# RWKV matrices right behind the z tiles, twelve gate tiles instead of fourteen beside the substitution, and a step's small gate operations ahead of the shift rows

## The chip, the cores and the metric

One core of one Trainium2 chip. The metric is the device time of one execution in microseconds, as the median of the runs. The profile is one further execution; its rows give times in us from the start of its span.

## What is computed

One step of a one-layer decoder for 256 new prompt tokens behind 16 meta tokens, and for 8 running sequences with one token each. One input projection `P = rmsnorm(h) @ w_in` feeds two branches. They are merged by sigmoid gates, and a product-key expert mixer (PEER) follows. All is float32.

```python
# DeltaNet branch, in chunks of the sequence
A = strict(kb @ k.T * decay) + I          # unit lower triangular
u, w = solve(A, [v * beta, kb * exp(G)])
v_new = u - w @ S
o = (q * exp(G)) @ S + tril(q @ k.T * decay) @ v_new
S = S * exp(G_last) + (k * exp(G_last - G)).T @ v_new
# RWKV-7 branch, token by token (the kernel solves it in chunks too)
S = S * w + (S @ a) b^T + v k^T ;  y = S @ r
# merge
m = sigmoid(P_gate_a) * (o_dn @ w_up_dn) + sigmoid(P_gate_b) * (o_rw @ w_up_rw)
h = h + m @ w_out
h = h + peer(rmsnorm(h))                  # top 16 of 128 x 128 experts per head, gathered rows
```

Here `g = -exp(a_log) * softplus(alpha + dt_bias)` and `beta = sigmoid(...)` come from eight small columns of the projection. For these the kernel needs `exp` and `log` on a 128 x 16 tile.

## The kernel before

The kernel is written per engine, with semaphores by hand. Each engine has one instruction list in a fixed order. TensorE (`pe`), ScalarE (`act`), VectorE (`dve`) and GpSimd (`pool`) compute, and SyncE (`sp`) issues nearly all transfers in one queue. Line 1428 is the matmul helper, line 1846 the activation helper: nearly all matmuls and activations carry these lines. A float32 matmul appears as two MATMUL records, each with its weight load. The sequence is three chunks of 96 tokens (NCH = 3, TC = 96, with padding), and the 8 sample tokens stand behind them in the same tiles (296 columns, or 264 without padding and meta tokens). PSUM has eight banks, called 0 to 7.

The work around the change, in order:

- **Projections** (`project`, line 1446): tiles of 128 output columns, each 8 matmuls over the 8 slices of the model dimension. Order: r, kr, vr, wag (the RWKV rows), then two q tiles, then 14 transposes that give the last token-shift rows (lines 1487 to 1490), two q tiles, and twelve products of the low-rank gates (lines 1495 to 1501: the first eight read 64 rows of the array, the last four 128). Then come k, v and z, with small matmuls of both branches between.
- **ScalarE at that place** (lines 1880 to 1909): 14 scalings of the RWKV rows (`mix`), copies of the shift rows from banks 4 to 7, tanh and sigmoid of the low-rank inputs (`wag_act`), the first q tile out, exponentials of `gtmp`, `bt`, `alog`, the second q tile out, the logarithm of `gtmp`, two more q tiles, then the sigmoids of the low-rank products. A function that is not in the loaded table needs an ACT_TABLE_LOAD. VectorE makes `gtmp` (lines 2144 to 2148) behind its fourteen parts of `mix`. Its line 2149 waits for the logarithm.
- **Middle** (lines 1549 to 1643). TensorE: z tile 0; the q norms spread back over rows (8-row products); 12 matmuls for the decay matrices (`gb_ready`, banks 4, 5, 7); the k norms spread back; z tile 1; the six DeltaNet matrix pairs (`kq_ready`, banks 0 to 5); six sample transposes (banks 6, 7); six groups of token transposes (banks 6, 7 in turn, so each waits for ScalarE's copy of the one before the last); z tile 2; six groups of RWKV row transposes; z tile 3; then `rw_matrix`: 12 groups with k (`rwm_ready`), half a gate tile, the key sum in bank 7, and 12 groups with b (`rwb_ready`). VectorE masks each result (lines 2286 to 2320). The last six groups need all of `rwb_ready`, as their result overwrites the b vectors.
- **Triangular inverses.** All 36 unit lower triangular matrices of 96 x 96 are inverted. The 32 x 32 diagonal blocks go out through DRAM by SP (`emit_blocks_in`), 108 blocks one per partition. VectorE inverts them by substitution in 31 steps (lines 2331 to 2341). SP brings them back (`emit_blocks_out`: one transfer out, nine in). Around the substitution VectorE runs the two halves of the sample state update `sample_rwkv` (line 602, nine instructions of 128 x 1024). The first needs `svp` (sixteen small transfers of SP, issued once the token rows are copied) and `strw` (two loads behind them, lines 466 to 477). TensorE meanwhile runs the gate tiles of the list `FILL` (line 1260, `fill_tile`, banks 6 and 7 in turn), fourteen of them. ScalarE takes each out through a sigmoid.
- **Coupling** (`inv_turn`, `inv_left`, `inv_once`, `inv_twice`, lines 1652 to 1704): nine units of four matrices join the blocks, pipelined over TensorE, ScalarE and VectorE. Units 0 to 2 are DeltaNet (chunks 0, 1, 2), 3 to 8 RWKV. VectorE makes `inv_c` (line 2350) behind the second half of the sample state.
- **Chunks** (line 1752): chunk after chunk, both branches' states. Chunk 0 begins once all nine units are done (`inv_z_used`). VectorE copies the first right side, `v_dn`, to `r_buf` (line 2445), and with it signals `dn_r_done`. SP waits for that signal before the sixteen small transfers of the sample result (line 501), since these overwrite `v_dn`'s place. Two gate tiles (g3's third and fourth) stand at the end of chunks 0 and 1.
- **Weights.** Slots of 2 MB; g0 to g3 share slot 0. `IN_PARTS` (line 251) cuts g1, g2 and g3 into parts, each of which is fetched as soon as its columns of the tile group before are used.

Behind it follow the merge and the output projection (to about 402 us) and the expert mixer, whose gathers and weighting run to the end of the span.

## Time and profile before

| | |
|---|---|
| three runs, median (lowest to highest) | 1148.66 us (1147.56 to 1153.62) |
| the profiled execution: its time / its span | 1150.32 / 1148.6 us |
| TensorE busy | 982.6 us (86%), x3667 |
| VectorE busy | 706.5 us (62%), x1870 |
| ScalarE busy | 264.1 us (23%), of it 22 table loads 28.2 us |
| GpSimd busy | 521.4 us (45%) |
| mean granted TensorE clock | 0.978 |

The span is the time from the first to the last instruction of the profiled execution. Its time is 1.7 us more. A busy TensorE is modelled from its instructions, and is not TensorE at its peak. The granted clock is given as a share of 2.4 GHz, and has two levels, 1.00 and 0.50.

### The profile page before, as it was taken

How to read it: one execution, taken by the hardware profiler on the slowest of the kernel's cores; microseconds unless marked ns; L12 is line 12 of the kernel's file. 1: busy time of each engine (PE TensorE's matmuls, PEld its weight loads, DVE VectorE, ACT ScalarE, POOL GpSimd, SP SyncE). 2: the span in 40 equal slices, each digit the busy share in tenths (PEclk: the TensorE clock that was granted, in tenths of full speed). 3: DMA queues.
4: the chain of work that ended last, by engine and by line, in shares of the span. 5: the costliest groups of instructions: out<-in, count | busy, mean ns of one | idle time of the engine just before them, and what ended most of it. 6: DMA issues, size and time to landing. Idle time of an engine off the chain costs nothing.

```text
span 1148.6 us, 11115 instructions
## 1 busy us (share of the span) xinstructions
PE 982.6 (86%) x3667; PEld 549.7 (48%) x3667; DVE 706.5 (62%) x1870; ACT 264.1 (23%) x635; POOL 521.4 (45%) x583
## 2 busy tenths in 40 slices
PE   6999998999999998988987777777777777777787
PEld 5886676889987447654442222222222222222221
DVE  2025862983466338883775775776686676677543
ACT  2147544023251012220131111111122111111111
POOL 2000100000000016577577677777767777777763
PEclk9998989998999998998999999999999999999999
DMA  9342022463165319999999999999999999999996
GB/s 288 110 153 74 1 76 50 135 171 82 40 208 208 110 46 405 407 371 353 409 406 403 409 409 409 406 408 408 408 388 410 409 409 410 405 409 404 395 371 263
DMA packets 121862, 334.24 MB, mean 291 GB/s; under 512 B 19119, under 2 KB 36370, under 8 KB 121542
## 3 DMA queue, kind: packets, MB, share of 16 engines
q0 software_dynamic: 76032, 276.86, 61.2%
q1 hardware_dynamic: 45642, 56.64, 15.2%
q8 instruction: 30, 0.49, 0.2%
q14 instruction: 26, 0.21, 0.0%
q10 hardware_dynamic: 132, 0.04, 0.0%
HBM read 326.99 MB, written 5.74 MB: 290 GB/s over the span
## 4 chain that ended last, share of the span: by engine, by line
PE 31%; DMA 28%; DVE 23%; POOL 9%; issue 5%; ACT 3%; ACTq 0%; DVEq 0%; POOLq 0%
PE bank L1428 29%; DMA sb_all<-in_peer_u,idx 22%; POOL sb_all L591 9%; DMA sb_all<-in_peer_v,idx 6%; DVE sb_all L1148 6%; ACT sb_all L1846 2%; DVE sb_all L1126 1%; DVE sb_all L1124 1%; DVE sb_all L1128 1%; DVE sb_all L2337 1%; DVE sb_all L2334 1%; DVE key_i L1096 1%; DVE sb_all L1089 1%; ACT L1846 1%; DVE key_i L1090 1%
## 5 line engine op out<-in xcount | busy, mean ns | idle before, releaser
L1428 PE MATMUL bank<-sb_all 128*128 128x512 f32 (+19 forms) x3390 | 952.3, 433 | 145.8 <-DMA sb_all<-in_peer_v,idx 135.6
L1428 PEld LDWEIGHTS bank<-sb_all 128*128 128x128 f32 (+8 forms) x3390 | 522.9, 182 | 569.7 <-DMA sb_all<-in_peer_v,idx 320.4
L1148 DVE CUSTOM_DVE_ANT_0 sb_all<-sb_all,bank 128x1024 f32<-128x1024 f32 x264 | 314.8, 1220 | 186.5 <-DMA sb_all<-in_peer_u,idx 186.0
L591 POOL DMA_INDIRECT sb_all<-in_peer_u,idx x264 | 252.6, 957 | 212.4 <-issue 161.1
L591 POOL DMA_INDIRECT sb_all<-in_peer_v,idx x264 | 254.6, 965 | 88.8 <-issue 63.8
L1846 ACT ACTIVATE sb_all<-sb_all 128x128 f32<-128x128 f32 (+9 forms) x367 | 145.1, 421 | 561.7 <-PE bank L1428 368.6
L1846 ACT ACTIVATE sb_all<-bank 128x264 f32<-128x264 f32 (+18 forms) x175 | 76.7, 455 | 305.2 <-PE bank L1428 272.0
L627 POOL MEMSET sb_all<- 128x512 f32 x1 | 0.5, 524 | 140.9 <-PE bank L1428 140.9
L1418 POOL MEMSET sb_all<- 128x3456 f32 x1 | 3.0, 2984 | 129.1 <-DVE sb_all L2248 129.1
L2129 DVE SCALAR_TENSOR_TENSOR sb_all<-sb_all 128x288 f32<-128x288 f32 x14 | 6.1, 514 | 61.2 <-ACT sb_all L1846 61.2
L1846 ACT ACT_TABLE_LOAD x22 | 28.2, 1283 | 7.5 <-DVE sb_all L2269 3.9
L1148 DVE DVE_READ_ACCUMULATOR2_ANT sb_all<- 128x1 f32 x264 | 21.7, 82 | 0.0
L2199 DVE SCALAR_TENSOR_TENSOR sb_all<-sb_all 128x288 f32<-128x288 f32 x36 | 16.0, 504 | 6.7 <-ACT sb_all L1846 6.6
L1061 DVE TENSOR_TENSOR sb_all<-sb_all,bank 128x512 f32<-128x512 f32 (+1 forms) x6 | 4.1, 683 | 25.0 <-PE bank L1428 25.0
L1126 DVE TENSOR_TENSOR sb_all<-sb_all 128x864 f32<-128x864 f32 x17 | 18.0, 1059 | 0.6
L1124 DVE TENSOR_TENSOR sb_all<-sb_all 128x864 f32<-128x864 f32 x17 | 18.0, 1059 | 0.6
L1128 DVE TENSOR_REDUCE sb_all<-sb_all 128x16 f32<-128x864 f32 x17 | 17.9, 1055 | 0.6
L1234 DVE SCALAR_TENSOR_TENSOR sb_all<-sb_all 128x1024 f32<-128x1024 f32 x8 | 10.3, 1285 | 12.6 <-DMA sb_all<-in_peer_v,idx 12.6
L2309 DVE TENSOR_TENSOR sb_all<-bank,sb_all 96x192 f32<-96x192 f32 x12 | 4.1, 340 | 19.5 <-PE bank L1428 19.5
L1420 POOL MEMSET sb_all<- 108x1024 f32 x1 | 1.0, 952 | 31.7 <-DVE sb_all L2295 31.7
L1846 ACT ACTIVATE sb_all<-bank,sb_all 96x128 f32<-96x128 f32 (+5 forms) x39 | 13.4, 415 | 6.3 <-PE bank L1428 5.5
L1086 DVE MAX8 sb_all<-sb_all 128x8 f32<-128x128 f32 x34 | 8.2, 284 | 10.5 <-ACT sb_all L1846 10.5
(237 smaller groups left out, 403.5 us busy)
## 6 DMA issues: line engine op xcount, KB each, us to landing
sb_all<-in_w_in SPq DMA_DIRECT2D x8, 2048.0 KB, 8.1
sb_all<-in_peer_wq SPq DMA_DIRECT2D x4, 2048.0 KB, 17.3
sb_all<-in_w_in SPq DMA_DIRECT2D x6, 1024.0 KB, 4.9
sb_all<-in_peer_u,idx POOLq DMA_INDIRECT x264, 10.8
sb_all<-in_peer_v,idx POOLq DMA_INDIRECT x264, 11.0
out<-sb_all SPq DMA_DIRECT2D x8, 512.0 KB, 3.9
sb_all<-in_w_out SPq DMA_DIRECT2D x2, 2048.0 KB, 8.6
sb_all<-in_x_prompt SPq DMA_DIRECT2D x4, 512.0 KB, 4.4
```

Of the source, the lines that this page charges most:

```text
L591: pool.indirect_dma_start(ring[at % 8], None, table[0], bass.IndirectOffsetOnAxis(ap=idx[:, c:c + 1], axis=0)).then_inc(landed[at % 8], 16)
L1089: k(v.match_replace(curm[:, x, :], best[:, x, 0:8], src[:, x, :], NEG))
L1090: k(v.max_index(key_i[:, PT * x:PT * x + 8], best[:, x, 0:8], src[:, x, :]))
L1096: k(v.max_index(key_i[:, PT * x + 8:PT * x + 16], best[:, x, 8:16], curm[:, x, :]))
L1124: k(tt(onehot, iota.unsqueeze(1).broadcast_to([128, PT, NCAND]), row(posf, 128, PT, NCAND), ALU.is_equal))
L1126: k(tt(onehot, onehot, cidx.unsqueeze(1).broadcast_to([128, PT, NCAND]), ALU.mult))
L1128: k(v.tensor_reduce(eidf, onehot, AX, ALU.add))
L1148: v.tensor_tensor_reduce(uring[i % 8], uring[i % 8], x, 1.0, 0.0, ALU.mult, ALU.add, hdot[:, u % 2, j:j + 1]).then_inc(u_free, 1)
L1428: return nc.tensor.matmul(out, lhsT, rhs, start=start, stop=stop, **kw)
L1846: return nc.scalar.activation(out, in_, func, **kw)
L2199: step(stt(x, pre[:, f, j:j + NP], pc("conv", 12 * j + f), x, ALU.mult, ALU.add))
L2334: step(tt(t, ublk[:, 0:k, k].unsqueeze(2).broadcast_to([108, k, n]), vblk[:, k, k:32].unsqueeze(1).broadcast_to([108, k, n]), ALU.mult))
```

## The change

Six things, all in the order of work:

1. **Small gates** (ScalarE, VectorE): VectorE makes `gtmp` ahead of its fourteen parts of `mix`. ScalarE does the three exponentials and the logarithm directly behind its fourteen scalings, ahead of the shift rows, and takes the four q tiles out in one go.
2. **z tile 1** stands between and behind the decay matrices in bank 6, in four pieces of two slices. The sample transposes stand between the DeltaNet matrices. z tile 2 (bank 6) comes ahead of the token transposes, which now go to banks 0 to 5. z tile 3 (bank 7) comes directly behind them.
3. **The RWKV matrices** come directly behind z. The row transposes stand between the second six of them. The first six with b follow; then the key sum, half a gate tile and the last six. VectorE copies the key sum after all of them.
4. **Twelve gate tiles** beside the substitution. g3's first and second tile come behind the coupling loop and in chunk 0 (banks 0 and 3). g3 is fetched whole, once g2 is used and the blocks are back.
5. **Coupling by chunks**: the nine units go chunk by chunk (each DeltaNet and both RWKV). Chunk 0's first product starts after the seventh unit. The last `inv_twice` comes behind gate tile 0.
6. **No copy of the first right side**: TensorE reads `v_dn`; `dn_r_done` counts from chunk 1, so SP's sample result transfers wait for chunk 1.

The diff, cut to its core:

```diff
-        UNITS_INV = [(g, q) for g in range(3) for q in range(3)]
+        UNITS_INV = [(g, q) for q in range(3) for g in range(3)]
...
-        IN_PARTS = {"g1": (256,), "g2": (256,), "g3": (128, 128)}
+        IN_PARTS = {"g1": (256,), "g2": (256,)}
...
             step(fn(view(E + 4096, 2 * NX), view(E + 4096, 2 * NX), ACT.Sigmoid))
+            step(fn(gates(12), gates(12), ACT.Sigmoid))
...
-        FILL = [(name, f) for name in ("g0", "g1", "g2") for f in range(4)] + [("g3", 0), ("g3", 1)]
+        FILL = [(name, f) for name in ("g0", "g1", "g2") for f in range(4)]
...
             for c in range(NCH):
                 for h in range(DH):
                     ins = mm(psv((4, 5, 7)[c], 128, TC, at=TC * h), gbc[0:TC, 4 * c + h, :], incl[0:TC, :])
                 ins.then_inc(gb_ready.sem, 1)
-            for f in range(4):
-                pe.wait_ge(qk_mul.sem, qk_mul.at(f + 1))
-                mm(psv(f, 128, NC), to_rows[0:8, 4 + f, :], qk_norm[0:8, :]).then_inc(k_back.sem, 1)
+                z_tile(1, 6, 2 * c, 2 * c + 2)
+            key_back(0)
+            key_back(1)
+            z_tile(1, 6, 6, KT)
+            key_back(2)
+            key_back(3)
             pe.wait_ge(dec_exp.sem, dec_exp.at(2 * NCH))
-            project("z", T0, banks=4, part=(1, 2))
...
+                if n >= 1:
+                    sample_rows(n - 1)
+            sample_rows(5)
+            pe.wait_ge(svt_ready.sem, svt_ready.at(5))
+            z_tile(2, 6, 0, KT)
             for n in range(6):
-                if n < 2:
-                    pe.wait_ge(svt_ready.sem, svt_ready.at(5 + n))
-                else:
-                    pe.wait_ge(tok_ready.sem, tok_ready.at(n - 1))
+                pe.wait_ge(kq_used, n + 1)
...
+            z_tile(3, 7, 0, KT)
...
-            pe.wait_ge(proj_used, 30)
             for n in range(12):
-                if n >= 6:
+                if n < 6:
+                    pe.wait_ge(tok_ready.sem, tok_ready.at(n + 1))
+                else:
+                    rw_rows(n - 6)
                     pe.wait_ge(rwm_used, n - 5)
                 rw_matrix(n % 6, kb, n // 6, n % 6 // 2, n % 2).then_inc(rwm_ready.sem, 1)
...
+            for n in range(6):
+                pe.wait_ge(rwm_used, n + 7)
+                rw_matrix(n, bb, 0, n // 2, n % 2).then_inc(rwb_ready, 1)
             pe.wait_ge(prw_ready.sem, prw_ready.at(6))
             mm(psv(7, 128, 32), ones, sdv[:, 2, :]).then_inc(kq_sum.sem, 1)
+            fill_tile(0, KT // 2)
+            for n in range(6):
+                pe.wait_ge(rwb_used, n + 1)
+                rw_matrix(n, bb, 1, n // 2, n % 2).then_inc(rwb_ready, 1)
             fill_tile(KT // 2, KT)
...
+            for u in range(NU + 2):
+                if u < NU:
+                    inv_turn(u)
+                if 1 <= u < NU + 1:
+                    inv_left(u - 1)
+                if u >= 2:
+                    inv_once(u - 2)
+                if u >= 3:
+                    inv_twice(u - 3)
+            pe.wait_ge(inv_z_used, 7)
+            right_side(0).then_inc(rw_r, 1)
+            pe.wait_ge(inv_x_used, NU)
+            gate_tile(0, 0)
+            inv_twice(NU - 1)
             for c in range(NCH):
...
                 for h in range(DH):
-                    ins = mm(psv(1, TC, 128, at=128 * h), xTm(4 * c + h), r_buf[0:TC, 128 * h:128 * h + 128])
+                    r_h = r_buf[0:TC, 128 * h:128 * h + 128] if c > 0 else v_dn[0:TC, 0, 128 * h:128 * h + 128]
+                    ins = mm(psv(1, TC, 128, at=128 * h), xTm(4 * c + h), r_h)
                 ins.then_inc(dn_u, 1)
+                if c == 0:
+                    gate_tile(1, 3)
                 pe.wait_ge(rw_r_done, c + 1)
+                pe.wait_ge(inv_z_used, NU)
...
             for f in range(14):
                 fn(mix[:, f, 0:NP], prw[:, f, 1:1 + NP], scale=omu[:, f:f + 1]).then_inc(mix_part.sem, 1)
+            act.wait_ge(ln_done, 1)
+            step(fn(gtmp, gtmp, ACT.Exp, scale=-1.0))
+            step(fn(bt, ba[:, :, 0:4], ACT.Exp, scale=-1.0))
+            step(fn(alog, alog, ACT.Exp))
+            step.sync()
+            fn(gtmp, gtmp, ACT.Ln, bias=1.0).then_inc(ln_done, 1)
...
-            evacuate([pre[:, 0, 3 + PAD:3 + NC]])
...
+            evacuate([pre[:, f, 3 + PAD:3 + NC] for f in range(4)])
...
+                if c == 0:
+                    gate_out(0, 0)
+                    act.wait_ge(inv_sum.sem, inv_sum.at(NU))
+                    gate_out(1, 3)
+                    act.wait_ge(yv_ready, 1)
+                    act.wait_ge(strw_sent, 32)
...
                 if c == 0:
                     dve.wait_ge(tok_ready.sem, tok_ready.at(6))
-                    v.tensor_copy(r_buf[0:TC], v_dn[0:TC, 0, :]).then_inc(dn_r_done, 1)
```

## Rows read from the trace of the kernel before

**Rows 1.** Chain of waits in order of time, 60 to 480: start, length, what, records

```profile
93.36 51.50 PE bank L1428 x190
...
242.69 1.15 DVE sb_all L606
```

**Rows 2.** Timeline of ScalarE, 74 to 102: start, length, engine, line, operation, [idle before]

```profile
74.10 6.07 ACT L1846 ACTIVATE sb_all<-sb_all 128x288 f32<-128x288 f32 x14
...
81.59 1.80 ACT L1846 ACTIVATE sb_all<-bank 9x512 f32<-9x512 f32 x4 [1.42 <-PE bank L1488]
...
83.41 1.28 ACT L1846 ACT_TABLE_LOAD   x1
...
88.52 0.56 ACT L1846 ACTIVATE sb_all<-sb_all 128x16 f32<-128x16 f32 x3
...
91.50 1.28 ACT L1846 ACT_TABLE_LOAD   x1
...
101.00 0.42 ACT L1846 ACTIVATE sb_all<-bank 128x296 f32<-128x296 f32 x1 [0.57 <-PE bank L1428]
```

**Rows 3.** Timeline of TensorE, 82 to 100, columns as in rows 2

```profile
82.48 9.90 PE L1428 MATMUL bank<-sb_all 128*128 128x280 f32 x40
...
93.36 7.12 PE L1428 MATMUL bank<-sb_all 64*128 64x296 f32 x15 [0.97 <-ACT sb_all L1846]
```

**Rows 4.** Busy time by stretch: length, each engine's, TensorE clock, DMA share, GB/s

```profile
94.40:101.20 6.80, 6.80 (x14) 4.20 (x13) 6.53 (x12) 3.36 (x9) 0.00 (x0) 0.50 0.41 157
...
118.30:121.60 3.30, 3.30 (x8) 2.33 (x7) 1.53 (x4) 0.00 (x0) 0.00 (x0) 0.50 0.00 0
...
155.80:166.00 10.20, 10.20 (x28) 7.36 (x27) 7.44 (x17) 5.04 (x8) 0.00 (x0) 0.50 0.01 2
...
275.30:285.50 10.20, 10.20 (x55) 10.20 (x55) 1.38 (x2) 1.19 (x2) 0.00 (x0) 0.50 0.83 208
...
285.50:326.40 40.90, 39.73 (x363) 38.12 (x362) 21.98 (x44) 11.74 (x25) 2.63 (x7) 1.00 0.17 60
```

**Rows 5.** Timeline of VectorE, 204 to 313

```profile
204.38 0.35 DVE L2319 TENSOR_TENSOR sb_all<-bank,sb_all 96x192 f32<-96x192 f32 x1 [0.98 <-PE bank L1428]
...
207.96 1.23 DVE L606 TENSOR_TENSOR sb_all<-sb_all 128x1024 f32<-128x1024 f32 x1
...
272.81 0.42 DVE L2361 TENSOR_TENSOR sb_all<-sb_all,bank 96x256 f32<-96x256 f32 x1 [0.46 <-PE bank L1428]
...
295.19 0.69 DVE L2448 TENSOR_TENSOR sb_all<-sb_all,bank 96x512 f32<-96x512 f32 x1 [7.67 <-PE bank L1428]
...
307.41 0.67 DVE L2371 TENSOR_REDUCE sb_all<-sb_all 8x8 f32<-8x512 f32 x1
...
312.24 0.68 DVE L2448 TENSOR_TENSOR sb_all<-sb_all,bank 96x512 f32<-96x512 f32 x1 [1.83 <-PE bank L1428]
```

**Rows 6.** Timeline of ScalarE: z tile 1 and a gate tile out

```profile
167.73 0.39 ACT L1846 ACTIVATE sb_all<-bank 128x264 f32<-128x264 f32 x1 [6.58 <-PE bank L1428]
...
213.47 0.39 ACT L1846 ACTIVATE sb_all<-bank 128x264 f32<-128x264 f32 x1 [3.17 <-PE bank L1428]
```

**Rows 7.** Timeline of TensorE: RWKV matrices and half a tile; first couplings

```profile
191.46 7.11 PE L1428 MATMUL bank<-sb_all 64*96 64x192 f32 x56 [0.48 <-ACT sb_all L1846]
...
254.29 0.92 PE L1428 MATMUL bank<-sb_all 96*96 96x96 f32 x8 [1.03 <-DVE sb_all L2350]
```

**Rows 8.** Timeline of TensorE's weight loads (PEld): decay matrices

```profile
153.89 3.48 PEld L1428 LDWEIGHTS bank<-sb_all 96*128 96x128 f32 x24 [0.40 <-issue]
```

**Rows 9.** Timeline of SyncE's queue: issues

```profile
181.47 10.68 SPq L471 DMA_DIRECT2D sb_all<-sb_all  x16
...
195.09 1.18 SPq L475 DMA_DIRECT2D sb_all<-in_state_rw  x2
...
278.26 11.52 SPq L505 DMA_DIRECT2D sb_all<-sb_all  x16
```

**Rows 10.** The loads from state_rw (strw), time from issue to landing

```profile
DMA to landing us min/median/max: 4.8/5.7/6.6
```

More of the change, by code:

```diff
@@ L1554, in _, with z_tile, key_back @@
                 mm(psv(f, 128, NC), to_rows[0:8, f, :], qk_norm[0:8, :]).then_inc(q_back.sem, 1)
+            def z_tile(f, b, first, last):
+                slot = wait_w(pe, "z")
+                for k in range(first, last):
+                    ins = mm(psv(b, 128, NX), wslot[slot][:, k, f * 128:(f + 1) * 128], xnT[:, k, T0:NC],
+                             start=k == 0, stop=k == KT - 1)
+                if last == KT:
+                    ins.then_inc(proj_ready, 1)
+                    tile[0] += 1
+            def key_back(f):
+                pe.wait_ge(qk_mul.sem, qk_mul.at(f + 1))
+                mm(psv(f, 128, NC), to_rows[0:8, 4 + f, :], qk_norm[0:8, :]).then_inc(k_back.sem, 1)
             pe.wait_ge(gb_in, 2)
+            pe.wait_ge(proj_used, 27)
             for c in range(NCH):
@@ L1695, in _ @@
             pe.wait_ge(inv_out, 16 * 9)
-            for u in range(NU + 3):
-                if u < NU:
-                    inv_turn(u)
-                if 1 <= u < NU + 1:
-                    inv_left(u - 1)
-                if 2 <= u < NU + 2:
-                    inv_once(u - 2)
-                if u >= 3:
-                    inv_twice(u - 3)
-            pe.wait_ge(proj_used, 43)
             def gate_tile(f, b):
@@ L1967, in _, with z_out @@
                 fn(dec[0:TC, 4 * c:4 * c + 4, :], dec[0:TC, 4 * c:4 * c + 4, :], ACT.Exp).then_inc(dec_exp.sem, 1)
-            evacuate(zs[1:2], ACT.Silu, NX, banks=4)
+            def z_out(f, b):
+                act.wait_ge(proj_ready, 27 + f)
+                fn(zs[f], psv(b, 128, NX), ACT.Silu).then_inc(proj_used, 1)
+                tile[0] += 1
+            z_out(1, 6)
             act.wait_ge(gexp_done.sem, gexp_done.at(1))
@@ L1990, in _ @@
                 fn((b_rw, k_rw)[n % 2][0:TC, n // 2, :], psv(6 + n % 2, TC, 512)).then_inc(prw_ready.sem, 1)
-            evacuate(zs[3:4], ACT.Silu, NX, banks=4)
-            for n in range(len(FILL) - 1):
+            for n in range(len(FILL)):
                 act.wait_ge(proj_ready, tile[0] + 1)
```

112 lines of the change are left out of this document (46 added, 66 removed).

## The prediction

> **What bounds the kernel now.** I read the chain of waits first. Up to 145 us it is one run of TensorE work (51.5 us in one piece), from about 208 to 254 us it is VectorE alone (the sample state, the 31 steps of the substitution, the sample state again), after that TensorE again [rows 1]. So until 335 us a microsecond counts only where TensorE waits or runs slowly, or where it moves the start of VectorE's block. Everything behind hangs on the mixer's end, so I pass a gain there on one to one.
>
> Next the timelines of ScalarE and TensorE around 80 to 101 us. TensorE reaches the low-rank products at 90.3 us (40 records from 82.48 for 9.90 us, of which the last 8 are four products at 0.49 us), waits 0.97 us at 93.36 for ScalarE's first sigmoid, and its twelfth product is out at 101.00 [rows 2, 3]. Then the granted clock by stretch: 0.50 (1.2 of 2.4 GHz) in 94.4 to 101.2, 118.3 to 121.6, 155.8 to 166.0 and 275.3 to 285.5, and 1.00 between the last of these and 326.4 [rows 4]. Each follows work that fills little of the array: products over 64 or 8 rows, or small ones with waits.
>
> In the middle, VectorE stands ready for the RWKV matrices while TensorE does transposes and z tiles, loses 0.98 us before the last six, and starts on the sample state at 207.96 [rows 5]. The fourteen gate tiles at 3.56 us [rows 6] lie beside its 46 us, so TensorE waits only 1.03 us for the couplings at 254.29 [rows 7].
>
> **Front: four ScalarE operations ahead of the shift rows.** ScalarE's fourteen scalings end at 80.17 (74.10 + 6.07). Then, with 1.30 us for a table load: load and three exponentials 1.86, load and logarithm 1.5, shift rows 1.80, load and tanh 1.8, load and sigmoid 1.8: 88.9 [rows 2]. The logarithm I take at 0.2, tanh and sigmoid at 0.5 each, by the 0.56 of the three exponentials. Four copies of 0.3 bring it to 90.2, or until TensorE's last q tile. One table load of the five (83.41 the first, 91.50 the last) is gone, and the sigmoid's table is already there when the first product arrives at 90.8. The wait of 0.97 goes, and twelve products at 0.49 us end at 96.2 instead of 101.0: **4.8 us**. What is behind the moved operations: the shift rows end at 85.4 instead of 83.4, and TensorE asks for them at 90.3; two small output transfers on SP start 2 us later, and SP has nothing to do until 90. VectorE's three small operations move ahead of its fourteen, where it waits for ScalarE; cost nothing, else 0.6. Uncertain is the clock. Eight of the products still read 64 rows. If one stretch as long as that at 118.3 (3.3 us) stays at 0.50, it costs 1.7 [rows 4]. I take 0.7 off: **4.1** (1.0 to 4.9). VectorE and ScalarE wait for TensorE's tiles behind this, so they follow.
>
> **Middle, first part: z tile 1 between the decay matrices.** Before, TensorE does 12 decay products (weight loads 153.89 + 3.48 us), four key products in low clock, then the z tile, which ScalarE takes at 167.73, when the DeltaNet matrices start [rows 4, 6, 8]. The tile's work is the same. At full clock the new order gives 153.85 + 3.5 + 3.6 + 4 x 0.5 = 162.9, VectorE's last multiplication 0.5 and its copy, so 163.7: 4.0 us gained. With the clock as before nothing is gained. As full-array work now stands inside the weak stretch, I expect one short stretch of low clock (1.7) instead of 10.2 us: **2.5** (0 to 4.1).
>
> **Middle, second part: to the sample state.** I count from the start of the DeltaNet matrices, T = 0; before, VectorE's sample state begins at 40.3. Now: six matrix pairs 3.9 (192 columns at the gate tile's rate of 3.56 / 8 for 264, so 0.32 a product) and six groups of sample transposes 2.9 between them, a group taken at a little under 0.5, z 3.6, six groups of token transposes at 0.5 in banks of their own, z 3.6: 17.0. Twelve matrices at 0.42 with six row transposes between, about 8; six more 2.4; the sum and half a gate tile 2.1; the last six 2.4; VectorE's last six pairs 3.2: 35.3 [rows 5, 6, 7]. But VectorE also needs the sample states, behind SP's queue: ScalarE's six copies of token rows, three pairs at 1.7 behind the second z tile, are out at T + 16.1, then sixteen issues 10.7, their landing 2.9, then the two loads (0.6 between them, 6.6 to land at most): T + 36.9 [rows 9, 10]. **So 3.4 us**, not 5.0 (2 to 4.5); the transfer becomes the last of the waits. The copy of the key sum moved to VectorE's end costs 0.2 of that.
>
> VectorE's block of 46.3 us is unchanged and leads to T + 83.2. TensorE ends its 11.5 remaining gate tiles at T + 73. It has nothing to do for some 8 us, until SP's transfers have brought the blocks back and the first transposes can start.
>
> The price of the two tiles moved: before, the loop's last sums come at 272.8, chunk 0 begins at 274.33, and with one gate tile it ends at 294.3, half of it in low clock [rows 4, 5, 7]. In the stretch at full clock behind it, 363 records took 40.9 us; less two tiles (7.1 us, 32 records) that is 0.102 us each [rows 4]. Chunk 0 has 120 records beside its gate tile: 12.2 + 3.6. From 272.8, with two tiles more: 272.8 + 15.8 + 7.1 = 295.7. That is 1.4 us later, the tiles' 7.1 being paid by 1.5 of gap and 4.2 of clock. Copies of ScalarE that TensorE waited for are covered by a tile now (minus 0.7), and a stretch of low clock may remain (0.3 x 1.7). Sum: **minus 1.2** (plus 2 to minus 5).
>
> The removed copy of VectorE was also SP's signal for sixteen transfers [rows 9]. They now go at 295.9 in the old count, take 11.5 and land by 310; VectorE wants them at 307.41, and its three further microseconds then touch what it has to do at 312.24, where TensorE has 1 us to spare [rows 5]. **Minus 0.3** (0 to minus 1.1). One more activation behind the mixer, 0.4 us, lies beside TensorE's work there: nothing. The third and fourth parts of g3 came after the blocks before; now all of g3 does, and is wanted some 20 us later: nothing.
>
> **Sum.** 4.1 + 2.5 + 3.4 - 2.0 - 1.2 - 0.3 = 6.5 us. The profiled execution took 1150.32, 1.7 over the median of 1148.66. 1150.3 - 6.5 = 1143.8; on the median's scale **1142.2**.
>
> **A page against the trace.** From one ScalarE table to the next function the rows show 1.28 us of load and about 0.02 beside it [rows 2]. The Trainium skill ("ScalarE: Activation LUTs", What ACT_TABLE_LOAD costs) adds a drain of about 1.38 us to a load, 2.66 in all. It speaks against putting two loads ahead of the shift rows; the trace does not agree with it.
>
> **Rivals.**
> - The first chunk pays: low clock stays over its 10 us in spite of the tiles. Another 4 us are lost: gain 2.5, 1146. For it: the products there are small, and 275.3 to 285.5 stayed low although TensorE counts as busy. Against: two runs of 16 full-array records stand in it. 0.17.
> - Slower, by the idle time before the inversion: the low clock it brings lasts through all nine units and the first gate tile, since small products do not lift it. The place is the loop; 9 x 1.2 + 3.6 = 14.4 instead of 2.0, and the sum turns to minus 5.9: 1154.6. It decides if the clock is still 0.50 after the fourth unit; from the seventh on all gain is gone. For it, the same 10.2 us. Against: the same loop kept 1.00 from 254 to 274. 0.06.
> - Clock rises everywhere: the front's 4.8, the middle's 4.0, inversion minus 1: gain 10, 1138.5. 0.14.
> - ScalarE is late: a table change ahead of a waiting operation costs as much again as its load. With 1.3 more for each of four, the sigmoid ends at 94.1, TensorE waits 3.8 us where it waited 1, and its products end at 100 or, in low clock, 102: 4.1 becomes minus 1, gain 1.4, 1147.3. Against it: load and next operation stand together in every row. 0.03. (It is the drain of the Trainium skill's page, above.)
> - My forecast, gain 4 to 9: 0.60, of which 0.42 above the threshold.
>
> A measurement of this kernel tells about 0.5% (5.7 us) from no change. Faster: 0.42 + 0.14 = 0.56. Slower: 0.06. Within: 0.38. The range for 8 in 10 takes the forecast's band and half of the rivals at either side, 1137.5 to 1148.3.
>
> **What would show it.** Right: no wait of TensorE between 90 and 96 us and its k tile there by 100; four ScalarE table loads from 80 to 90; VectorE's sample state starting about 10 us earlier, ended by a transfer; a TensorE gap of some 8 us with low clock behind it; chunk 0 ending 6 to 7 us earlier. Wrong: ScalarE's first sigmoid after 92 us; the sample state earlier by under 6 us; inversion over 24 us; chunk 0 in low clock for long; anything past 340 us that takes the gain back.

## The result, and the profile after

The changed kernel takes 1160.24 us (median of four runs, 1158.21 to 1162.13) beside 1148.11 us of the kernel before on the same chip (four runs, 1145.13 to 1153.62). The ratio is 1.0096 with an interval of 1.0065 to 1.0128: slower, outside the range of the prediction. All ratios here leave disturbed executions out; for e1 below that leaves out two at 1163.4 us, which are themselves what that experiment is about. The profiled execution took 1158.21 us, its span 1156.4, against 1150.32 and 1148.6 before. So the rows below explain a difference of 7.8 us; the medians lie 12.1 us apart, as the execution profiled here is its kernel's quickest and that of the kernel before lies 2.2 us above the median. The other 4 us are scatter between executions, for which no row stands here.

The page of the kernel after: span, the TensorE clock in 40 slices of 29 us each, the table loads.

```profile
span 1156.4 us, 11112 instructions
...
PEclk9999999965999998999999999999999999999999
...
L1878 ACT ACT_TABLE_LOAD x21 | 26.9, 1283 | 7.5 <-DVE sb_all L2308 3.9
```

One table load is gone, as the change says. The clock line has a hole, "65", in the ninth and tenth slices: 231 to 289 us. Before, no slice was below 8. That is the stretch to look at, but the way to it comes first.

**The front.** ScalarE's timeline of the kernel after (start, length, engine, line, operation, idle before):

```profile
82.32 1.28 ACT L1878 ACT_TABLE_LOAD   x1
83.61 0.42 ACT L1878 ACTIVATE sb_all<-sb_all 128x16 f32<-128x16 f32 x3
84.05 1.28 ACT L1878 ACT_TABLE_LOAD   x1
85.35 0.22 ACT L1878 ACTIVATE sb_all<-sb_all 128x16 f32<-128x16 f32 x1
85.47 1.79 ACT L1878 ACTIVATE sb_all<-bank 9x512 f32<-9x512 f32 x4
87.27 1.28 ACT L1878 ACT_TABLE_LOAD   x1
...
89.03 1.28 ACT L1878 ACT_TABLE_LOAD   x1
...
93.05 3.59 ACT L1878 ACTIVATE sb_all<-bank,sb_all 128x296 f32<-128x296 f32 x8 [0.29 <-PE bank L1429]
```

Four loads, each followed by its operation 0.01 to 0.02 us later. Now ScalarE waits for TensorE (0.29 and 0.70 us) and no longer the other way round. TensorE of the kernel after:

```profile
83.08 1.69 PE L1489 MATMUL bank<-sb_all 128*9 128x128 f32 x14
84.61 55.47 PE L1429 MATMUL bank<-sb_all 128*128 128x280 f32 x230
140.67 1.47 PE L1542 MATMUL bank<-sb_all 128*11 128x128 f32 x12 [0.59 <-ACT sb_all L1878]
```

and the same two places before:

```profile
80.95 1.69 PE L1488 MATMUL bank<-sb_all 128*9 128x128 f32 x14
...
145.43 1.47 PE L1541 MATMUL bank<-sb_all 128*11 128x128 f32 x12 [0.59 <-ACT sb_all L1846]
```

One piece of 55.47 us without a wait. From the shift rows to the small products behind v it takes 57.59 us, where it took 64.48: 6.9 us less. In the span only 4.8 of them show, as this execution came to the shift rows 2.1 us late. TensorE's first projections started 0.4 us later (14.17, after a wait for their weights, instead of 13.73) and then took 17.0 us instead of 15.3, at a clock of 0.72 in 14 to 20 us where it was 1.00 before. That lies ahead of everything the change touches, and the profiles of e3, e4, e8 and e9 below have the same 0.72 there while those of the other six have 1.00.

**The middle.** The DeltaNet matrices start 18.4 us behind the small products (22.3 before), and VectorE's sample state 39.0 us behind them (40.2 before):

```profile
159.11 2.85 PE L1429 MATMUL bank<-sb_all 128*96 128x192 f32 x8 [0.89 <-DVE sb_all L2314]
```

```profile
194.46 0.35 DVE L2356 TENSOR_TENSOR sb_all<-bank,sb_all 96x192 f32<-96x192 f32 x1 [2.56 <-PE bank L1429]
...
198.15 1.23 DVE L606 TENSOR_TENSOR sb_all<-sb_all 128x1024 f32<-128x1024 f32 x1
```

So the sample state starts 9.8 us earlier than in [rows 5], and in the first 200 us nearly all that was hoped for is there.

**The inversion.** TensorE of the kernel after, from its last gate tile on, and the busy time by stretch (length, busy time of TensorE, its weight loads, VectorE, ScalarE, GpSimd, then the clock):

```profile
235.82 2.16 PE L1429 MATMUL bank<-sb_all 128*128 128x264 f32 x9
242.27 1.49 PE L1682 MATMUL bank<-sb_all 96*96 96x96 f32 x8 [4.28 <-DMA sb_all<-inverse]
244.48 1.59 PE L1429 MATMUL bank<-sb_all 96*96 96x96 f32 x8 [0.72 <-DVE sb_all L2389]
...
253.53 3.27 PE L1429 MATMUL bank<-sb_all 96*96 96x96 f32 x24
...
257.40 3.28 PE L1429 MATMUL bank<-sb_all 96*96 96x96 f32 x24
```

```profile
240.70:285.50 44.80, 42.51 (x274) 39.63 (x275) 13.05 (x28) 11.77 (x28) 0.00 (x0) 0.51 0.21 73
285.50:330.00 44.50, 44.50 (x388) 42.31 (x386) 19.67 (x39) 11.02 (x23) 1.44 (x3) 1.00 0.33 96
```

The gate tiles end at 237.98, then nothing until the blocks are back 4.28 us later. The clock is at 0.50 before the first transpose, from 240.5 on, and stays there until 284.9, some 44 us; in the row's 44.8 us TensorE is busy for 42.51. It comes back 4.6 us into gate tile 0, which starts at 280.2. A unit comes every 3.87 us (253.53 to 257.40) instead of 2.17. VectorE adds one sum a unit. The next row is the eighth of the nine sums, the last inside the loop; then comes the ninth, behind gate tile 0, then chunk 1's first right side:

```profile
277.69 0.42 DVE L2400 TENSOR_TENSOR sb_all<-sb_all,bank 96x256 f32<-96x256 f32 x1 [1.30 <-PE bank L1429]
...
286.68 0.42 DVE L2400 TENSOR_TENSOR sb_all<-sb_all,bank 96x256 f32<-96x256 f32 x1 [8.26 <-PE bank L1429]
...
304.79 0.69 DVE L2486 TENSOR_TENSOR sb_all<-sb_all,bank 96x512 f32<-96x512 f32 x1 [7.67 <-PE bank L1429]
```

The account. The first line has points of time, the others lengths, each the difference of two rows (the merge's first product is at 339.00 before and 348.60 after). The eighth sum stands at 272.81 before; the ninth comes 0.7 us later there. For the DeltaNet matrices before, ScalarE's row at 167.73 is taken; by TensorE's own first record of them (167.5) the two lines would be -3.7 and -1.4.

| stretch | before | after | difference |
|---|---|---|---|
| up to the shift rows | 80.95 | 83.08 | +2.1 |
| to the small products behind v | 64.48 | 57.59 | -6.9 |
| to the DeltaNet matrices | 22.3 | 18.4 | -3.9 |
| to the sample state | 40.2 | 39.0 | -1.2 |
| VectorE's block, to the first couplings | 46.3 | 46.3 | 0 |
| first couplings to the eighth sum | 18.5 | 33.2 | **+14.7** |
| from there to chunk 1 | 22.4 | 27.1 | **+4.7** |
| chunk 1 to the merge | 43.8 | 43.8 | 0 |
| merge to the end of the span | 809.6 | 807.8 | -1.8 |

The sum is +7.7, and the spans differ by 7.8. The question for the experiments is whether the +14.7 and most of the +4.7 are the clock alone, what brought it down, and why it did not come back.

### The profile page after: what moved, and what is told of

Its sections match the earlier page's. It is cut to its first block, busy times and chain, and to the rows that moved or that the text cites. A ratio compares the mean times of both kernels' runs of the same rounds, so it can differ in the third digit from the quotient of the medians.

```text
span 1156.4 us, 11112 instructions
## 1 busy us (share of the span) xinstructions
PE 989.3 (86%) x3667; PEld 556.2 (48%) x3667; DVE 706.3 (61%) x1869; ACT 263.7 (23%) x635; POOL 518.7 (45%) x583
## 4 chain that ended last, share of the span: by engine, by line
PE 35%; DMA 29%; DVE 19%; POOL 11%; issue 5%; ACT 1%; SPq 0%; DVEq 0%; POOLq 0%
PE bank L1429 33%; DMA sb_all<-in_peer_u,idx 15%; DMA sb_all<-in_peer_v,idx 13%; POOL sb_all L591 11%; DVE sb_all L1149 5%; DVE sb_all L1125 1%; DVE sb_all L1127 1%; DVE sb_all L1129 1%; DVE sb_all L2376 1%; DVE sb_all L2373 1%; DMA sb_all<-in_w_in 1%; ACT sb_all L1878 1%; DVE key_i L1097 1%; DVE sb_all L1090 1%; DVE key_i L1091 1%
## 5 line engine op out<-in xcount | busy, mean ns | idle before, releaser
L1429 PE MATMUL bank<-sb_all 128*128 128x512 f32 (+18 forms) x3390 | 958.0, 436 | 145.4 <-DMA sb_all<-in_peer_v,idx 134.7
L1429 PEld LDWEIGHTS bank<-sb_all 128*128 128x128 f32 (+8 forms) x3390 | 527.0, 185 | 569.7 <-DMA sb_all<-in_peer_v,idx 319.4
L1878 ACT ACTIVATE sb_all<-sb_all 128x128 f32<-128x128 f32 (+10 forms) x368 | 145.2, 420 | 561.0 <-PE bank L1429 369.5
L2400 DVE TENSOR_TENSOR sb_all<-sb_all,bank 96x256 f32<-96x256 f32 x9 | 3.8, 419 | 31.8 <-PE bank L1429 31.8
L2238 DVE SCALAR_TENSOR_TENSOR sb_all<-sb_all 128x288 f32<-128x288 f32 x36 | 16.0, 505 | 5.0 <-ACT sb_all L1878 5.0
## 6 DMA issues: line engine op xcount, KB each, us to landing
sb_all<-in_peer_wq SPq DMA_DIRECT2D x4, 2048.0 KB, 17.2
```

What stands on the lines that cost most here:

```text
L1429: return nc.tensor.matmul(out, lhsT, rhs, start=start, stop=stop, **kw)
L1878: return nc.scalar.activation(out, in_, func, **kw)
L2238: step(stt(x, pre[:, f, j:j + NP], pc("conv", 12 * j + f), x, ALU.mult, ALU.add))
```

## The experiments

Ten kernels ran, each beside the kernel before on the same chip: e1 to e4 on one chip, e5 to e8 on a second, e9 and e10 on a third. The x8 or x24 of a row counts records, of which a float32 product has two. The shapes of a row are the weights (rows times columns of the array), then the operand that runs through them: 128*128 128x264 has 264 columns running through a full array.

### e1: the gap filled

```diff
                 ins.then_inc(inv_sum.sem, 1)
 
             pe.wait_ge(rwb_used, 12)
+            for n in range(10):
+                mm(psv(3, 128, NX), ones, xnT[:, n % KT, T0:NC])
             pe.wait_ge(inv_out, 16 * 9)
```

Ten products of a gate tile's shape, whose result nobody reads, stand ahead of TensorE's wait for the blocks.

> The changed kernel with ten full-array products (ones times a slice of the normed input, 264 columns, 4.45 us, result unused, bank 3) in TensorE's empty stretch behind the twelfth gate tile; it computes ten products more than the changed kernel and leaves nothing out. Clock theory (the empty 4.3 us drop the granted clock to 0.50, and the small coupling products cannot lift it again): the coupling loop keeps 1.00 and takes 2.17 us a unit instead of 3.87, both moved tiles run at 3.56 us; chunk 0 ends some 17 us earlier than the 304 of the changed kernel; time 1141 to 1144, ratio to the kernel before 0.994 to 0.997. Rival, the two moved tiles and the new loop order are the cost and the low clock only goes with them: still low for most of 244 to 285, ratio 1.007 to 1.013. Rival, chunk by chunk order of the units makes a unit longer whatever the clock: clock at 1.00 and a unit over 3 us.

Measured: eight executions, 1138.3 to 1141.9 in six and 1163.4 in two, with nothing between; median 1141.15, ratio 0.9918 (0.989 to 0.9947). One kernel, two times, 22.7 us apart. The profile fell on one of the two long ones:

```profile
235.83 9.06 PE L1429 MATMUL bank<-sb_all 128*128 128x264 f32 x40
...
247.59 0.92 PE L1429 MATMUL bank<-sb_all 96*96 96x96 f32 x8 [1.35 <-DVE sb_all L2391]
```

```profile
248.60:286.00 37.40, 37.40 (x251) 35.19 (x250) 8.40 (x22) 10.71 (x26) 0.00 (x0) 0.50 0.14 51
```

With the gap of 4.28 us cut to 0.48 the clock fell all the same, now inside the first unit, behind transposes, a wait of 1.35 us for the couplings and their first products. Then it stayed low for 37.4 us in which TensorE was not idle for a moment. So the empty stretch is not needed: in some executions the clock falls where only waits of 0.5 and 1.4 us stand. No profile of a short execution exists, but the mean granted clock of each execution is on record: 0.973 and 0.968 in the two long ones, 0.989 to 0.994 in the six short ones. From 0.973 and 0.991 I estimate 42 us more of low clock in the long profiled one, worth some 21 us at half clock, close to the 22.7. That the two moved tiles or the new order of units are the cost, the first rival, doesn't fit the six short executions, which have both.

### e2 and e3: parts of the change by themselves

e3 is the kernel before with part 1 (the small gates). e2 is the changed kernel with parts 4 to 6 taken back; its core:

```diff
-        UNITS_INV = [(g, q) for q in range(3) for g in range(3)]
+        UNITS_INV = [(g, q) for g in range(3) for q in range(3)]
-        IN_PARTS = {"g1": (256,), "g2": (256,)}
+        IN_PARTS = {"g1": (256,), "g2": (256,), "g3": (128, 128)}
-        FILL = [(name, f) for name in ("g0", "g1", "g2") for f in range(4)]
+        FILL = [(name, f) for name in ("g0", "g1", "g2") for f in range(4)] + [("g3", 0), ("g3", 1)]
...
+                    v.tensor_copy(r_buf[0:TC], v_dn[0:TC, 0, :]).then_inc(dn_r_done, 1)
```

> Parts 1 to 3 of the change alone: front and middle as changed, and from the gate tiles on as before (fourteen tiles, g3 in parts, units group by group, the copy of the first right side). Clock theory: TensorE's tiles cover VectorE's block, no empty stretch over 1.5 us, loop at 1.00; coupling begins some 9.5 us earlier than 254.3 and everything behind follows: 1138 to 1141, ratio 0.991 to 0.994. Rival (the middle's new order is what fails): ratio 0.998 or more.

> Part 1 alone. Taking the changed kernel's profile at its word: the products of the low-rank gates come without a wait and without low clock, the shift is 4.8 us and with the second low stretch at 118 gone 6.5: ratio 0.994 to 0.996. If a gain at the front is swallowed further on (VectorE's block reached with TensorE's tiles late): 0.998 to 1.000.

Measured: e3 1144.25 us (twelve executions), ratio 0.9947 (0.9929 to 0.9966), which by the ratio is 6.1 us of the 1150.41 that the kernel before took there. e2 1139.1 (six), ratio 0.9904 (0.9872 to 0.9937), which is 11.0 us. The same kernel again on another chip (e10, below) gave 0.9929 (0.9904 to 0.9955). So parts 1 to 3 are a gain, and part 1 is the larger half of it. TensorE of e2:

```profile
239.76 7.06 PE L1428 MATMUL bank<-sb_all 128*128 128x264 f32 x31
246.66 0.83 PE L1681 MATMUL bank<-sb_all 96*96 96x96 f32 x8
247.82 0.89 PE L1428 MATMUL bank<-sb_all 96*96 96x96 f32 x8 [0.34 <-ACT sb_all L1869]
```

```profile
246.00:268.00 22.00, 20.54 (x258) 19.20 (x257) 10.42 (x28) 11.39 (x28) 0.00 (x0) 1.00 0.26 72
269.70:279.90 10.20, 10.20 (x54) 10.20 (x53) 1.38 (x2) 1.97 (x4) 0.00 (x0) 0.50 0.79 198
```

Fourteen tiles reach to 246.7, the blocks are there, and the loop runs at 1.00. Its first chunk has the 10.2 us of low clock that [rows 4] have. How that stretch ends bears on the whole argument. In the kernel before the clock is back at 285.5, and these are all of TensorE's products from there to 290.4, where chunk 0's gate tile follows:

```profile
L1428 PE MATMUL bank<-sb_all 96*96 96x64 f32 x47 | 4.1, 248 | 0.0
L1428 PE MATMUL bank<-sb_all 96*128 96x128 f32 x8 | 1.1, 275 | 0.0
L1428 PE MATMUL bank<-sb_all 96*96 96x128 f32 x2 | 0.6, 384 | 0.0
```

So the chunk's own products, over 96 rows, brought the clock back, 5 us ahead of the first product over the whole array. e2 (back at 279.9) and e10 (276.4) show the same. In that stretch 32 of 53 records have 128 columns running through; in the coupling loop none has more than 96.

### e4: parts 4 to 6 by themselves

The kernel before with the edits of parts 4 to 6 (the reverse of the diff above, on the old front and middle).

> Parts 4 to 6 alone: twelve gate tiles under the substitution, two behind the loop, on top of the kernel before. Clock theory: TensorE is empty for some 7 us ahead of the loop, the clock falls there and stays at 0.50 to the end of the first moved tile; loop 35 us instead of 20, chunk 0 ends 17 to 19 us later: 1163 to 1168, ratio 1.013 to 1.018. Rival, the clock falls only by chance of phase: ratio 1.00 to 1.005 with the loop at 1.00.

Measured: 1168.79 us (four executions, 1165.25 to 1171.3), ratio 1.0154 (1.0113 to 1.0194).

```profile
254.25 1.49 PE L1659 MATMUL bank<-sb_all 96*96 96x96 f32 x8 [6.55 <-DMA sb_all<-inverse]
```

```profile
251.00:294.00 43.00, 39.03 (x264) 36.91 (x265) 14.68 (x29) 11.82 (x28) 0.00 (x0) 0.50 0.24 80
```

The loss sits in parts 4 to 6, which were not run apart from each other: +1.5% alone, -0.7 to -1.0% for parts 1 to 3, +0.96% together. It needs no new front or middle.

### e5: thirteen tiles instead of twelve

```diff
-        IN_PARTS = {"g1": (256,), "g2": (256,)}
+        IN_PARTS = {"g1": (256,), "g2": (256,), "g3": (128,)}
-        FILL = [(name, f) for name in ("g0", "g1", "g2") for f in range(4)]
+        FILL = [(name, f) for name in ("g0", "g1", "g2") for f in range(4)] + [("g3", 0)]
...
-            gate_tile(0, 0)
+            gate_tile(1, 0)
...
-                if c == 0:
-                    gate_tile(1, 3)
```

> The changed kernel with thirteen gate tiles under the substitution (g3's first fetched in a part of its own) and one, g3's second, behind the coupling loop in bank 0. The empty stretch should shrink from 4.3 us to under 1. Clock theory: loop at 1.00 in most executions, and the one tile behind the loop keeps chunk 0 above 0.50 for most of it: 1136 to 1140, ratio 0.988 to 0.992. If only a fully dense start keeps the clock: low in the loop, 1155 or more, in part or all of the runs.

Measured: 1156.11, 1157.65, 1158.88, 1156.49, 1158.35 us and, once, 1138.03; the kernel before 1147.08 (median of 21). No ratio with an interval came of it; that of the medians is 1.0087. From the profile of the 1156.11:

```profile
243.67 0.84 PE L1681 MATMUL bank<-sb_all 96*96 96x96 f32 x8 [1.46 <-DMA sb_all<-inverse]
245.49 1.59 PE L1428 MATMUL bank<-sb_all 96*96 96x96 f32 x8 [0.98 <-DVE sb_all L2383]
```

```profile
245.00:284.00 39.00, 38.51 (x259) 36.45 (x260) 9.82 (x25) 10.88 (x27) 0.00 (x0) 0.50 0.16 55
```

Two waits of 1.46 and 0.98 us, with 0.84 us of transposes between, stand where e2 had 0.34. Five of six executions are some 19 us longer than the sixth; their mean granted clock is 0.972 to 0.974, the sixth's 0.990. So this lies on an edge. One tile of 3.6 us, thought of as a filler to be moved at will, decides over five times its own length.

### e6: both waits covered

e1, and six more such products behind the first unit's transposes.

```diff
                 if u < NU:
                     inv_turn(u)
+                if u == 0:
+                    for n in range(6):
+                        mm(psv(3, 128, NX), ones, xnT[:, n, T0:NC])
```

> As e1, with six more full-array products behind the first transposes, so that TensorE has no wait of 1.3 us for the couplings either; sixteen products more than the changed kernel in all. Two of eight executions of e1 took 1163 us. Theory: whether the clock falls just ahead of the loop depends on how the two waits lie to the chip's own timing; with both covered no execution is at 1163, all lie at 1139 to 1144. Rival, the 1163 come from something else (the transfers, the chip): they stay at 1 or 2 in 8.

Measured: nine executions, all between 1140.9 and 1143.6, median 1142.66, ratio 0.9947 (0.993 to 0.9965). None is near 1163. By itself that is weak: if two in eight fell, nine without one would come about one time in thirteen by luck, and e1 ran on another chip. TensorE and the stretch:

```profile
243.78 0.54 PE L1682 MATMUL bank<-sb_all 96*96 96x96 f32 x4 [0.36 <-DMA sb_all<-inverse]
244.15 2.86 PE L1429 MATMUL bank<-sb_all 128*128 128x264 f32 x12
```

```profile
240.00:320.00 80.00, 78.69 (x736) 73.59 (x734) 39.35 (x78) 24.80 (x56) 2.63 (x7) 1.00 0.33 99
```

VectorE of e6, the eighth sum and chunk 1's first right side:

```profile
265.62 0.42 DVE L2405 TENSOR_TENSOR sb_all<-sb_all,bank 96x256 f32<-96x256 f32 x1 [0.46 <-PE bank L1429]
...
289.21 0.69 DVE L2491 TENSOR_TENSOR sb_all<-sb_all,bank 96x512 f32<-96x512 f32 x1 [7.67 <-PE bank L1429]
```

This is the changed kernel's tail at full clock. Its first couplings are at 247.18, so it is 18.4 us to the eighth sum, as before (18.5), with the units in the new order: the order costs nothing. From there to chunk 1 it is 23.6 us against 22.4: two more tiles, and no low clock in the first chunk either. Set beside the kernel after, 33.2 and 27.1, the clock's price is 14.8 + 3.5 = 18.3 us. The sixteen extra products (7.1 us of work at the gate tile's rate) made the first couplings 1.1 us later: they stand 1.7 us behind the start of VectorE's first work for them here (245.49), and 0.6 in the kernel after (243.88). 18.3 less 1.1 is 17.2, and the two ratios, 1.0096 and 0.9947, lie 17.1 us apart.

### e7: can it be lifted inside the loop?

```diff
                 if u >= 3:
                     inv_twice(u - 3)
+                if u == 4:
+                    for n in range(10):
+                        mm(psv(7, 128, NX), ones, xnT[:, n % KT, T0:NC])
```

> The changed kernel, its empty stretch kept, with ten full-array products (bank 7, result unused) inside the loop behind the fifth turn of it. Theory, small products keep a clock that is up but cannot lift one that is down, full-array ones lift it: low from 240 until these products, then 1.00, units of 2.17 us from there to the end. Low work from 262 to 285 (23 us) becomes some 12, the products cost 5 to 9: 1152 to 1157. Rival, the loop lowers the clock of itself when it starts cold: low again within two units, 1165 or more.

Measured: 1155.0 us (seven executions, 1152.69 to 1157.78), ratio 1.0065 (1.0042 to 1.0089). The gap is as in the kernel after (4.59 us), and the clock falls as there, but:

```profile
241.80:262.00 20.20, 17.96 (x102) 16.38 (x103) 7.42 (x13) 5.18 (x12) 0.00 (x0) 0.50 0.47 161
262.00:310.00 48.00, 48.00 (x451) 44.92 (x450) 15.93 (x36) 13.79 (x29) 0.00 (x0) 1.00 0.18 45
```

The clock returned within the ten products over the whole array (from 257.8 to 264.6), 4.3 us into them, much as it returns 4.6 us into gate tile 0 in the kernel after. It then held 1.00 through the rest of the same 96 x 96 units and through chunk 0. The loop's products, which did not bring the clock back, keep it once it is up. This is the run that tells "the loop's products run slowly" from "the loop's products stay in the state in which they find the clock". What it is about the ten products isn't separated: they use all rows and columns of the array and run 264 columns through, and chunk 0 above shows that less than that can do.

### e8: the middle's two losses taken out

e2, with two groups of row transposes at a time ahead of the matrices with k, and the half gate tile moved behind the last six.

```diff
-                    rw_rows(n - 6)
+                    if n % 2 == 0:
+                        rw_rows(n - 6)
+                        rw_rows(n - 5)
                     pe.wait_ge(rwm_used, n - 5)
...
-            fill_tile(0, KT // 2)
...
-            fill_tile(KT // 2, KT)
+            fill_tile(0, KT)
```

> e2 (parts 1 to 3) with two edits of the middle: the RWKV row transposes two groups at a time, so that the matrix pairs over rows 0 to 63 and 64 to 127 stand next to each other again (a pair group took 0.82 us between transposes against 0.42 in a row), and the half gate tile moved behind the last six matrices, which VectorE waited 2.57 us for. Theory: 2.4 and some 2 us off VectorE's start, 1134 to 1136, ratio 0.985 to 0.988. If the matrices' time has nothing to do with their neighbours: 0.82 stays and the gain is 2 us or less.

Measured: 1143.2 us (twelve executions), ratio 0.9958 (0.9942 to 0.9975). The expected 0.985 to 0.988 is missed. It is slower than e2 by e2's ratio; the interval of the same kernel in e10 (0.9904 to 0.9955) overlaps it, so what is certain is that nothing was gained. The pairs do get cheaper. A row of the kernel after (one group of two products behind its transposes), then one of e8 (two groups):

```profile
180.22 0.89 PE L1429 MATMUL bank<-sb_all 64*96 64x192 f32 x4
```

```profile
182.06 0.90 PE L1428 MATMUL bank<-sb_all 64*96 64x192 f32 x8
```

But what follows in e8, on VectorE and on TensorE, is:

```profile
198.28 0.17 DVE L2353 COPY sb_all<-sb_all 64x32 f32<-64x32 f32 x1 [2.95 <-DMA sb_all<-in_state_rw]
...
198.70 1.23 DVE L606 TENSOR_TENSOR sb_all<-sb_all 128x1024 f32<-128x1024 f32 x1
```

```profile
209.89 4.31 PE L1428 MATMUL bank<-sb_all 128*128 128x264 f32 x12 [3.52 <-DMA sb_all<-in_w_in]
```

VectorE is ready 2.95 us before the sample states (`strw`) are there, so the sample state starts only 1.2 us earlier than in e2 (199.90). And TensorE waits 3.52 us (0.40 in e2) for g1's columns, whose transfer SP issues at 203.80, behind those of the blocks. There the clock is 0.55 in 209 to 212. With that the first couplings stand at 248.13, where e2 has 247.82: the 1.2 us are gone before the loop starts. The stretches of low clock are also longer in e8's profile, 6.8 us in the middle (3.4 in e2) and 13.7 from 267.3 on (10.2 in e2). Two small losses were taken out, and other waits stood close behind them.

### e9 and e10: a version that beats both

e9 is e5 with four products ahead of the wait for the blocks and four behind the first unit's transposes.

```diff
+            for n in range(4):
+                mm(psv(3, 128, NX), ones, xnT[:, n, T0:NC])
             pe.wait_ge(inv_out, 16 * 9)
...
                 if u < NU:
                     inv_turn(u)
+                if u == 0:
+                    for n in range(4):
+                        mm(psv(3, 128, NX), ones, xnT[:, n, T0:NC])
```

> The kernel with thirteen tiles beside the substitution and one behind the loop (e5), with four products of 128 x 264 over x that go nowhere ahead of TensorE's wait for the returned blocks, and four more behind the first unit's transposes, ahead of its wait for the couplings. They add 8 x 0.45 = 3.6 us, of which the two waits (1.5 and 1.0 in the run of e5) cover about 2.4. Theory (waits ahead of small products let the clock fall, and the small products cannot lift it again): no low clock between the six last RWKV matrices and the merge, every execution in the band of the one quick run of e5, 1138.0, plus about 1: 1137 to 1141, ratio about 0.990. Rival 1 (the quick run of e5 was chance and the tiles must stand beside the substitution): executions still fall in two groups, some at 1157. Rival 2 (the first chunk pays for the tile taken from it): no long low clock, but 1143 or more, later than the kernel with the front and the middle alone (e2).

> The kernel of e2 again (parts 1 to 3 of the change on the kernel before), beside e9 on the same chip, so that the two can be compared: ratio to before 0.990 as in e2, 1137 to 1143, one stretch of low clock in the first chunk and none in the loop. Theory: e9 is level with it or up to 4 us quicker, as e9 has no low clock in the first chunk. Rival 2 of e9: e9 is slower than this one.

Measured on one chip: e9 1138.94 us (six executions, 1136.57 to 1141.05), ratio 0.9903 (0.9878 to 0.9927); e10 1142.35 (six, 1138.52 to 1143.46), ratio 0.9929 (0.9904 to 0.9955). None of e9's is near 1157, where five of e5's six were; e5 itself did not run on this chip. Its stretch:

```profile
242.00:286.00 44.00, 44.00 (x446) 41.16 (x445) 16.66 (x36) 14.32 (x34) 0.00 (x0) 1.00 0.37 109
```

TensorE has no wait there at all. The expectation that no low clock would be left up to the merge fell: it is 0.50 from 316.1 to 319.4, as it is ahead of the merge in the profiles of all the others. e9's merge begins at 327.95, e10's at 330.27, that of the kernel before at 339.00. The intervals of e9 and e10 overlap. By medians and by these rows e9 is ahead, which agrees with the theory and doesn't prove it. Both beat the kernel before; against the changed kernel it is 1.7 to 1.9%, by their ratios and its 1.0096.

## Why the prediction was wrong, step by step

**The step that failed is "Inversion: minus 2.0 (0 to minus 4)".** It put 3.4 us on a unit for two units. A unit in low clock takes 3.87, and all nine of them ran in it, with the first 4.6 us of the gate tile behind: 14.7 + 3.5 = 18.2 us by the rows, 18.3 against e6. (Two units at 3.4 would have been minus 2.5, not minus 2.0.) The 3.4 rested on a weight load that doesn't double. It doesn't quite: a 96*96 load takes 0.280 us in the loop, 0.165 before, 1.7 times as long.

The text saw the idle time, and rightly said that it would lower the clock. What it assumed without a row was how the clock comes back. Its only ground, "the same loop kept 1.00 from 254 to 274", was no evidence: there the clock was up on entry. e7 shows both halves in one execution. The row that did bear on it was 275.3 to 285.5 in [rows 4], in which TensorE was busy throughout with small products and the clock stayed low for 10.2 us. The rival named exactly that row, and it speaks against a return within two units. But it doesn't carry the rival all the way either: at 285.5 the clock did rise, still among small products (see e2), and no row of the kernel before has low clock for longer than 10.2 us. That the loop's own products would leave it low for 44 us no row of that trace could show, as they had only run at 1.00 in it; the two units were a guess. The forecast also had the gap at 8 us, as it had TensorE's tiles end at T + 73; they ended at T + 78.9, and 4.3 us were enough.

**The rival "Slower, by the idle time before the inversion" is what happened**, with its place, its mechanism and its deciding point (0.50 still after the fourth unit). Its reason, that small products do not lift the clock, holds for the loop's products and not for chunk 0's. Its sum was short: 9 x 1.2 + 3.6 = 14.4 against 18.2, nearly all of it by the 3.4 instead of 3.87 a unit. The tile's 3.6 came out as 3.5.

**Front, +4.1 (1.0 to 4.9): the mechanism right, the size outside its range, 6.9.** ScalarE's order, four loads and the end of TensorE's wait are there. 4.8 was worked out at full clock, and 6.9 is measured from the shift rows. The difference is mainly the second stretch of low clock at 118.3 (3.3 us at 0.50, 1.65 of them lost), which went too, and for which nothing had been counted. Nor did 0.7 have to come off for the clock. With e3 at 6.1 us the front alone carries more than half of what parts 1 to 3 bring.

**Middle, first part, +2.5 (0 to 4.1): right, 3.9.** The low clock there lasts 3.4 us (158.6 to 162.0) instead of 10.2, and nearly all of it lies behind the start of the DeltaNet matrices, so that the second part pays for it.

**Middle, second part, +3.4 (2 to 4.5): over-sized, outside its range, 1.2.** The first RWKV matrix was to start at T + 17.0 and starts at T + 18.3 (177.44), by that low clock. The forecast also took 0.42 us for each group of RWKV matrices wherever it stands, from 56 records in a row [rows 7]. Between transposes one group takes 0.82 (the row at 180.22, until 181.04), so the six cost about 2.4 us more. The two make 35.3 into 39.0, the measured value; VectorE's wait of 2.56 us for the last six, which the half gate tile holds back, was in the 35.3. The term that was named as the limit, the transfer of `strw` at T + 36.9, was not it: by its issues (189.1 and 189.7) and the longest time to landing, 7.2 us, it was there by T + 37.8. e8 shows that it comes next, once the others go.

**First chunk and two tiles, minus 1.2 (plus 2 to minus 5): right at full clock.** e6 measures 23.6 us against 22.4, minus 1.2. "The first chunk pays" (0.17) fell with it: in e6 and e9, and in the kernel after once the clock was back, no low clock stood in the chunk.

**SP's sample result, minus 0.3: 0.** Its row in the kernel after:

```profile
317.41 0.68 DVE L2410 TENSOR_REDUCE sb_all<-sb_all 8x8 f32<-8x512 f32 x1 [0.32 <-DMA sb_all<-sb_all]
```

VectorE waits 0.32 us, and chunk 1 to the merge takes 43.8 us as before. That a gain ahead of the merge passes on one to one held to within 1.8 us: from the merge to the end it is 809.6 us before, 807.8 after, 809.5 in e9 and 809.3 in e10 (spans 1137.4 and 1139.6).

**ScalarE is late (0.03): fell.** Load and operation stand 0.01 to 0.02 us apart in four places. The Trainium skill ("ScalarE: Activation LUTs", What ACT_TABLE_LOAD costs) adds a drain of about 1.38 us to each load of 1.28. This trace agrees with the load and not with the drain.

**A page on the clock.** The rows: 42.51 of 44.80 us busy, clock 0.51. The Trainium skill ("TensorE: Matmul & The Clock Gate", What's actually happening) describes the low clock as the default of an idle engine, from which activity releases it. By that rule the loop, in which TensorE is busy nearly without a break, would have come back early, as the forecast had it. The trace does not agree for the loop, and does, after 10.2 us, for chunk 0 before: how busy the engine is by the profile was not all that decided, and by e7 the kind of products that kept it busy did.

What stays open: what in a product counts towards the clock, its rows, its columns, the columns that run through or its being a transpose (a part of the loop's are); no run changed one of them alone. e1's two groups lie 22.7 us apart, and the loop and chunk account for about 18. e1's long profile also has 6.8 us of low clock in the middle and 6.8 ahead of the merge where e6's has 3.4 each, at most 3.4 us of time; whether e1's short executions lacked them isn't known, as none was profiled. Which of the two uncovered waits brings the clock down in e5 isn't separated either, nor whether real gate tiles in place of the products that nobody reads would do as well in e9.

## What to carry to other kernels

Before work is moved away from the stretch ahead of a run of small products, look at what the clock will be on entry. Such a run can keep the clock it finds: this loop of 96 x 96 products did, high or low, so an uncovered wait at its door cost 18.3 us on a loop of 18.4, and not the length of the wait. Other small products (chunk 0's) came back by themselves after 7 to 10 us, so read it from a trace of your own loop. Cover the wait with products over the whole array, real ones where there are some, and leave a margin: at waits of 1 to 1.5 us the same kernel gave 1138 us once and 1157 five times. And when an operand comes through a queue, look where the next transfer in it stands before you bring its consumer forward.

## What was new about the hardware

- What the clock was on entry decided what it stayed: in one kernel the same 96 x 96 products ran at 0.50 for 20 us and, behind ten products of 128 x 264, at 1.00 for the rest of the loop (e7). In e1 the clock fell behind the first wait of 1.35 us and was 0.50 for 37.4 us, without an idle moment.
- Small is not all alike: chunk 0's products over 96 rows, most of them with 128 columns running through, raised the clock from 0.50 to 1.00 after 10.2 us (before, e2) and 6.8 us (e10), with no product over the whole array among them.
- One and the same program can fall on either side: six executions at about 1140.7 us and two at 1163.4 (e1), five at about 1157 and one at 1138 (e5). A profile of one execution shows only one of the sides.
- Two groups of RWKV matrices in a row take 0.90 us (e8), one by itself between transposes over all rows 0.82 to 0.89 (after). Their products read 64 rows each. Side by side two groups cost hardly more than one alone.
